# Neighbourhood attention with grid tokens in column order: two local key tiles per query tile, batches of two units, new bias layout

## The reference

```python
def neighbourhood_mixer(h_lat, h_ctx, p, need_ctx):
    ...
    kr = min(NA_ROWS_MAX, rows)                    # 8
    ...
    row_start = jnp.clip(r_idx - kr // 2, 0, rows - kr)
    col_start = jnp.clip(col - NA_COLS // 2, 0, GRID_W - NA_COLS)
    col_in = (col[None, :] >= col_start[:, None]) & (col[None, :] < col_start[:, None] + NA_COLS)
    ...
        s_loc = jnp.einsum('bqhd,brkhd->bhqrk', q_row, k_band).astype(jnp.float32) * ATTN_SCALE
        row_off = r0 + jnp.arange(kr) - r + NA_ROWS_MAX - 1
        bias = rpb[:, row_off][:, :, col_bias_idx].transpose(0, 2, 1, 3)
        s_loc = jnp.where(col_in[None, None, :, None, :], s_loc + bias[None].astype(jnp.float32), -jnp.inf)
        s_ctx = jnp.einsum('bqhd,bkhd->bhqk', q_row, k_c).astype(jnp.float32) * ATTN_SCALE
        s_all = jnp.concatenate([s_loc.reshape(B, NA_HEADS, GRID_W, n_loc), s_ctx], axis=-1)
        prob = jax.nn.softmax(s_all, axis=-1).astype(v_band.dtype)
        p_loc = prob[..., :n_loc].reshape(B, NA_HEADS, GRID_W, kr, GRID_W)
        o = (jnp.einsum('bhqrk,brkhd->bqhd', p_loc, v_band)
             + jnp.einsum('bhqk,bkhd->bqhd', prob[..., n_loc:], v_c))
...
    y_l = o.swapaxes(0, 1).reshape(B, S, D_MODEL) @ w_o
```

## Time and profile before

| | us |
|---|---|
| median of 3 runs | 3770.7 |
| lowest and highest | 3765.78, 3772.08 |
| span of the profiled execution | 3767.7 |
| TensorE busy in it | 3632.9 |
| VectorE, ScalarE, GpSimd busy | 2181.4, 1367.4, 830.9 |
| first scores of the neighbourhood attention, from the span's start | 1265.63 |
| its first transposes | 1276.84 |
| its last result written | 1426.8 |
| first matmul of the product behind it | 1429.22 |

### The profile page before, as it was taken

One profiled execution on the slowest core, in us unless ns is written; L12 is line 12 of the kernel. 1 busy time (PEld: TensorE's weight loads), 2 busy tenths in 40 slices (PEclk: granted clock), 3 DMA queues, 4 the chain that ended last, 5 costly groups with the idle time before them and its releaser, 6 DMA issues. The chain is left out here.

```text
span 3767.7 us, 53849 instructions
## 1 busy us (share of the span) xinstructions
PE 3632.9 (96%) x20043; PEld 2976.8 (79%) x20043; DVE 2181.4 (58%) x3423; ACT 1367.4 (36%) x2405; POOL 830.9 (22%) x588
## 2 busy tenths in 40 slices
PE   7999999999999999999999999999999998999998
PEld 5876788888878777777787888888878876687886
DVE  5748756566573564444436666556566628856445
ACT  4347541221243574222327622121224334523222
POOL 1500013223132111222220012213110008901222
PEclk9999999999999999999999999999999999999999
DMA  5234223332222212444310023323321240032322
GB/s 188 67 123 135 68 90 118 107 116 101 105 79 68 79 46 90 156 156 156 114 59 12 13 83 118 117 90 116 117 67 45 67 160 14 21 123 90 100 97 70
DMA packets 191993, 352.37 MB, mean 94 GB/s; under 512 B 42236, under 2 KB 43853, under 8 KB 191821
## 3 DMA queue, kind: packets, MB, share of 16 engines
q1 hardware_dynamic: 187693, 340.83, 27.4%
q10 hardware_dynamic: 4144, 9.44, 0.7%
HBM read 341.71 MB, written 16.92 MB: 95 GB/s over the span
## 5 line engine op out<-in xcount | busy, mean ns | idle before, releaser
L591 POOL TENSOR_TENSOR x<-x,scaled_buf 128x512 f32<-128x512 f32 (+1 forms) x360 | 493.4, 1387 | 2125.7 <-DVE scaled_buf L583 2125.1
L129 DVE TENSOR_TENSOR w_lo<-raw,w_hi 128x2048 fp32r<-128x2048 f32 x198 | 466.1, 2354 | 679.9 <-ACT w_hi L123 671.1
L123 ACT ACTIVATE w_hi<-raw 128x2048 fp32r<-128x2048 f32 x197 | 377.2, 1915 | 1286.4 <-PE psum L404 1284.0
L402 PE MATMUL psum<-hT_hi,w_hi 128*128 128x512 f32 (+1 forms) x1888 | 668.4, 354 | 2.9 <-issue 1.7
L403 PE MATMUL psum<-hT_lo,w_hi 128*128 128x512 f32 (+1 forms) x1888 | 665.1, 352 | 0.0
L404 PE MATMUL psum<-hT_hi,w_lo 128*128 128x512 f32 (+1 forms) x1888 | 664.7, 352 | 0.0
L402 PE MATMUL psum<-w_hi,uT_hi 128*128 128x512 f32 x1280 | 503.1, 393 | 0.1
L404 PE MATMUL psum<-w_hi,uT_lo 128*128 128x512 f32 x1280 | 498.6, 390 | 0.0
L403 PE MATMUL psum<-w_lo,uT_hi 128*128 128x512 f32 x1280 | 498.1, 389 | 0.0
L583 DVE TENSOR_TENSOR scaled_buf<-psum,gate 128x512 f32<-128x512 f32 x360 | 244.9, 688 | 328.0 <-PE psum L404 285.1
L402 PE MATMUL psum<-w_hi,hT_hi 128*128 128x512 f32 x1072 | 420.0, 392 | 4.4 <-issue 3.3
(11 more groups left out here) (292 smaller groups left out, 4883.5 us busy)
## 6 DMA issues: line engine op xcount, KB each, us to landing
raw<-in_w_mlp SPq DMA_DIRECT2D x64, 1024.0 KB, 5.3
raw<-in_ff_w SPq DMA_DIRECT2D x64, 1024.0 KB, 5.2
mod_wide<-in_w_mod SPq DMA_DIRECT2D x32, 1536.0 KB, 8.6
mod_wide<-in_w_mod SPq DMA_DIRECT2D x8, 3072.0 KB, 10.5
raw<-in_ssm_w_in SPq DMA_DIRECT2D x20, 1024.0 KB, 5.1
mod_slab<-in_w_mod SPq DMA_DIRECT2D x8, 2048.0 KB, 8.3
raw<-in_a_w_qkv SPq DMA_DIRECT2D x12, 1024.0 KB, 5.3
raw<-in_b_w_qkv SPq DMA_DIRECT2D x12, 1024.0 KB, 5.2
```

Source lines behind the costliest of these rows:

```text
L123: act.activation(K.w_hi[h][:, :, :], K.raw[h][:, :, :], ACT.Copy).then_inc(K.hi_done.h, 1)
L129: dve.tensor_tensor(K.w_lo[h][:, :, :], K.raw[h][:, :, :], K.w_hi[h][:, :, :].bitcast(F32), ALU.subtract).then_inc(K.lo_done.h, 1)
L402: pe.matmul(out, hi_a, hi_w, start=first, stop=False, **check)
L591: pool.tensor_tensor(x, x, K.scaled_buf[:, j % 2, :], ALU.add).then_inc(K.added.h, 1)
```

## The change

Grid tokens of this layer are numbered column by column. ScalarE writes them so into `feat` in `operand_stage` (`by_columns`). A key tile is then 16 grid columns with their 8 rows. The query tiles are shifted by half a tile against them: query tile t of 1 to 3 is the second half of tile t - 1 and the first half of tile t, and tile 0 is the first 8 and the last 8 columns. The window of such a query tile lies in two key tiles: t - 1 and t, or 0 and 3 for tile 0. The halves are put in place as the turned queries are evacuated (`turned_between`, two pieces an item, all four tiles of a group turned first). The attention has a stage of its own: a unit has two local and two context key tiles, 512 columns a head and one PSUM bank; units go in batches of two, with a step of transposes of batch s, scores of s + 2, weighted values of s - 1. The bias has zeros for the context columns, and its layout in HBM has changed. The way back to token order is in `window_split_stage`, feature by feature, and the product behind it takes features in order (`SplitFeed`).

```diff
@@ operand_stage, ScalarE
-                    out = feat[:, k % 2, t0 * P:(t0 + n) * P]
+                    out, turned = feat[:, k % 2, t0 * P:(t0 + n) * P], bank[:, 0:n * P]
+                    if by_columns and c == 0:
+                        out, turned = out.rearrange("p (c r) -> p r c", r=N_ROWS), turned.rearrange("p (r c) -> p r c", c=GRID_W)
...
@@ start_stage, SP and VectorE
-            sp.wait_ge(K.cleared.h, 1)
-            sp.dma_start(K.rel_table[:, 1:1 + REL_ROWS, REL_AT:REL_AT + REL_COLS], rpb).then_inc(K.rel_loaded.h, 16)
+            sp.dma_start(K.rel_in[:, :, :], rpb).then_inc(K.rel_loaded.h, 16)
...
-            link(dve.tensor_scalar(K.rel_table[:, :, :], K.rel_table[:, :, :], -1.0, None, ALU.mult))
+            dve.wait_ge(K.cleared.h, 1)
+            for r in range(N_ROWS):
+                ins = dve.tensor_scalar(K.rel_table[r // 4][:, r % 4, REL_AT:REL_AT + REL_COLS, :],
+                                        K.rel_in[:, N_ROWS - 1 - r:REL_ROWS - r, :].rearrange("h k c -> h c k"), -1.0, None, ALU.mult)
+            link(ins)
...
@@ bias: skewing, loading, masking
+def skew_bias(K, sp, p):
+    for head in (2 * p, 2 * p + 1):
+        for q0, q1, col0, kind in ((0, BLOCK_COLS, REL_AT + N_ROWS - 1, 0), (0, HALF_COLS, 2 * REL_AT - 1, 1),
+                                   (HALF_COLS, BLOCK_COLS, N_ROWS - 1, 1)):
+            src = bass.AP(tensor=K.rel_dram.tensor, offset=(head * REL_STEP + col0) * N_ROWS,
+                          ap=[[REL_STEP, N_ROWS], [-N_ROWS, q1 - q0], [1, 2 * P]])
+            sp.dma_start(K.skewed[head, kind, q0:q1].rearrange("c r x -> r c x"), src).then_inc(K.rel_loaded.h, 16)
...
+        sp.dma_start(bias_of(K, p)[:, m, 0::2, :], K.skewed[2 * p + m].rearrange("a c r x -> (c r) a x")).then_inc(K.g_loaded[p % 2].h, 16)
...
+    g = bias_of(K, p)[:, :, 0::2, :]
+    for m in range(2):
+        ins = pool.tensor_tensor(g[:, m], g[:, m], K.window_mask[:, :, :], ALU.add)
...
@@ turn_stage: ScalarE (VectorE likewise)
+                    pool.memset(bias_of(K, p)[:, :, 1, :], 0.0)
...
-                    act.wait_ge(K.src_turned.h, st0 + i + 1)
+                    act.wait_ge(K.src_turned.h, st0 + (turned_first[i] if turned_first else i + 1))
+                    for part, out in pieces(dst):
+                        ins = act.activation(out, blocks(i, part), ACT.Copy, scale=scale)
...
@@ window_attention_stage, in place of attention_stage with bias=True
+    def keys_of(t):
+        return (4, 5, 0, 3) if t == 0 else (t - 1, t, 4, 5)
...
+            def scores(b):
...
+                            if half == 0:
+                                pe.wait_ge(*upto(K.s_read, 2 * (v - 2) + m + 1))
+                            k = K.qkv[rows, first:second + 1:second - first, D + p * P:D + (p + 1) * P]
+                            mm = pe.matmul(bank_of(i, m)[:, half * LOCAL:(half + 1) * LOCAL], K.qkv[rows, t, p * P:(p + 1) * P], k,
+                                           start=half == 0, stop=True, skip_group_check=True)
...
+            def turns(b):
+                for i in range(2):
+                    pe.wait_ge(*upto(K.p_done, 2 * (2 * b + i) + 2))
+                    for m in range(2):
+                        c = 4 * b + 2 * i + m
+                        pe.wait_ge(*upto(K.pt_read[0], c - 2))
+                        for n in range(4):
+                            mm = pe.transpose(turning(c)[:, n * P:(n + 1) * P], K.p_win[:, b % 2, i, m, n * P:(n + 1) * P], K.ident[:, :])
...
+            for s in range(-2, NB):
+                if s >= 0:
+                    turns(s)
+                if s + 2 < NB:
+                    scores(s + 2)
+                if s >= 1:
+                    weighted(s - 1)
...
+            for s in range(-1, NB):                      # ScalarE
+                if s >= 0:
+                    copied(s)
+                if s + 1 < NB:
+                    probabilities(s + 1)
...
+                        dve.tensor_tensor_reduce(K.p_win[:, b % 2, i, m, :], bank_of(i, m)[:, :], g, 1.0, 3e38, ALU.add, ALU.min,
+                                                 K.win_min[:, b % 2, i, m:m + 1]).then_inc(K.s_read.h, 1)
...
+            for s in range(-2, NB):                      # VectorE
+                if s >= 1:
+                    inverse_sums(s - 1)
+                if s + 2 < NB:
+                    minima(s + 2)
+                if s >= 1:
+                    finish(s - 1)
...
@@ window_split_stage, in place of split_stage
+            for k in range(KD):
+                for src, at in pieces(k):
+                    ins = act.activation(at(grid(K.hT_hi, k)), src, ACT.Copy)
+                ins.then_inc(K.feat_hi.h, 1)
+            gate_evacuations(K, act, mm0, 1)
...
+                for src, at in pieces(k):
+                    ins = dve.tensor_tensor(at(grid(K.hT_lo, k)), src, at(grid(K.hT_hi, k)).bitcast(F32), ALU.subtract)
```

More of the change, by code:

```diff
@@ L1608, in turn_stage @@
     bank = lambda i: K.bank[(i - len(items)) % 8]
+    blocks = lambda i, part: bank(i).rearrange("p (a b) -> p a b", a=4)[:, :, part]
+    pieces = lambda dst: dst if isinstance(dst, list) else [(slice(0, P), dst)]
     with engines(K) as block:
@@ L1671, in _ @@
                 if i % 2 == 1:
-                    dve.wait_ge(K.src_turned.h, st0 + i + 1)
-                    dve.tensor_scalar(dst, bank(i).rearrange("p (a b) -> p a b", a=4), scale, None, ALU.mult)\
-                       .then_inc(K.src_read[1].h, 1)
+                    dve.wait_ge(K.src_turned.h, st0 + (turned_first[i] if turned_first else i + 1))
+                    for part, out in pieces(dst):
+                        ins = dve.tensor_scalar(out, blocks(i, part), scale, None, ALU.mult)
+                    ins.then_inc(K.src_read[1].h, 1)
                 if i == 7:
@@ L1686, in turn_stage, with attention_stage @@
     K.src_read[1].n += len(items) // 2
-def attention_stage(K, units, q_of, k_of, values, out, diff=False, bias=False, sink=False, mod=None, squares=False, context=None):
+def attention_stage(K, units, q_of, k_of, values, out, diff=False, sink=False, mod=None, squares=False):
     nc = K.nc
@@ L1718, in attention_stage @@
     with engines(K) as block:
[L1719 to L1727 removed]
+        if mod:
             @block.sync
@@ L1842, in probabilities @@
                 u = units[v]
-                if bias or sink:
+                if sink:
                     act.wait_ge(K.nm_done.h, at(K.nm_done, v))
```

273 lines of the change are left out of this document (200 added, 73 removed).

## The result

The changed kernel takes 3720.85 us (median of 4 runs, 3719.49 to 3722.64) where the kernel before takes 3770.26 beside it (4 runs, 3765.78 to 3772.08): a ratio of 0.9872, 95% interval 0.986 to 0.9884, 49.4 us less. The forecast was 3720 (3711 to 3734). The profiled execution has a span of 3717.7 us against 3767.7.

The account below looks back on a forecast made before the run. TensorE, busy 96% of the span, was taken to bound the kernel. Terms of -49.5, -4.8, +2.4, +0.2, +1.1 and +0.2 sum to -50.4: 3767.7 becomes 3717.3, plus 3.0 for the runs' median gives 3720 us, range 3711 to 3734.

Parts of the forecast that it names:

- Loop: Neighbourhood attention, first transposes to last result: TensorE sets the pace, 100.4 us where 149.9 stood, -49.5 us.
- hand-over: Attention loop: the fourth chunk of transposes waits for ScalarE's first bank copy, 0.1 us per batch, 1.6 in all.
- upper bound given for the period: Attention loop: two units' time scaled in plain proportion, changeovers too, 6.35 us against 6.2 by pieces.
- Fill: First scores to first transposes of the attention: 6.4 us against 11.2, with 1.5 charged for the lower clock, -4.8 us.
- Turn stage: Before the attention: scores wait for all evacuations, query tiles written in two pieces, +2.4 us, between +1.2 and +3.
- Start: Before layer 0: one VectorE operation on the bias table becomes eight, +1.1 us, bounds +0.5 and +3.
- Input stage: ScalarE writes the token order by columns for eight features; only the first delays the product, +0.2 us.
- rival 2: Input stage and split: scattered column writes are slow, four times as long, +3 and +4 us, 3727; chance 0.13.
- Split: After the attention: operands come feature by feature, the gate covers most of the first, +0.2 us, bounds 0 and +1.
- Rival 1: Attention loop: the banks pace it, hand-over 0.6 us a batch rather than 0.1, 8 more, 3728; chance 0.12.
- Rival 3: Attention loop: pauses keep TensorE at the half clock, 99 us more, 3819; chance 0.01.
- Rival 5: Cheaper yet: no half clock in the fill and no hand-over wait, -3 us and a little, 3716; chance 0.15.

Follow-up runs that it names:

- the extra copies: Changed kernel with one or three extra ScalarE copies into a spare buffer after each batch's four exponentials: 3723.8 us with one, 3734.2 with three.
- the copy in front: Changed kernel with one extra ScalarE copy into a spare buffer ahead of the first of each batch's four bank copies: 3729.8 us.
- the masks moved: Kernel before, with GpSimd's masks of the second and third head pair moved from the turn stage into the attention stage: ratio 1.0001.

## Why the prediction was right, and where it was not

- **Loop, -49.5 forecast, -50.3 measured.** Right by its own steps: transposes 1.91 + 0.1 hand-over (1.99), scores 1.95 (1.93), weighted 1.80 (1.80), inverse 0.54 (0.53), period 6.3 (6.25). That TensorE sets the pace is shown by the extra copies, that the hand-over stands exactly at its edge by the copy in front. The 0.8 us missed lie in the period, 6.25 against 6.3, sixteen times; the ends came out as charged. The second turn starts 0.35 late and the third another 0.49 (periods of 4.27 and 6.74), together the 0.8 of the sum, and the last weighted group waits 1.08 for 1.2. The upper bound given for the period, 6.35, should be 6.40 by its own rule; nothing hung on it.
- **Fill, -4.8 forecast, -6.4 measured.** The step that failed is the charge of 1.5 us for a lower clock: the clock stayed at 1.00 from the first scores on, and its last pause, 1.63 us just before them, did not lower it. The 4.9 of the sum before that charge was right (4.82). The reason given for before's length was wrong in its weight: the operation of 2.75 us accounted for 1.04, the rest is the three groups in one set of banks and the half clock. What the prediction did not see is that the same operation stood in the loop of before five more times.
- **Turn stage, +2.4 forecast, +1.6 measured.** Mechanism as forecast: the scores wait for all of VectorE's items, and its late low part sits in front of them. The size was off because the stretched low part fell from 3.02 to 2.60 us, as the lower bound had allowed, and the high part came 0.6 late, not 0.9. The terms named also add up to 2.3, not 2.4.
- **Start, +1.1 forecast, +2.9 measured.** The mis-sized term is the eight operations: 0.52 us each and 4.14 together, not 0.29 and 2.3. The price was taken from a 128-column read of PSUM in contiguous order; these read SBUF with a step of 31 words over 16 partitions. The +3 of the range held it.
- **Input stage, +0.2 forecast, +1.1 measured.** This is rival 2's mechanism at a small size: 1.74 times as long, not four. The Trainium skill, "Advanced Engine Details and Errata", memory cachelines, says that a new 16-byte line at each element costs a penalty; by that rule the written side had to be slower, and the traces agree, with 1353 against 778 ns. The step that failed is the claim that only the first feature delays the product. In the table above 0.5 of it is hidden, because layer 0 ran that much shorter: the profile of before has the half clock behind layer 0's attention (0.58 from 446 to 450 us), that of after has not.
- **Split, +0.2 forecast, -0.1 measured.** The pieces did get slower than charged, ScalarE's 384 columns with a step of 64 words 916 ns and 128 columns 436, but the gate covers the first and 2.7 us of product each later one. For the first it does so with nothing to spare: its low part ended 2.26 us after the last result, at 1377.36, where 1.6 had been charged, and the product started at 1377.46. The rows, in order of the two engines:

```profile
L2175 ACT ACTIVATE hT_hi<-qkv 128x384 fp32r<-128x384 f32 x8 | 7.3, 916 | 0.0
L2184 DVE TENSOR_TENSOR hT_lo<-qkv,hT_hi 128x384 fp32r<-128x384 f32 x8 | 7.1, 887 | 0.0
```

- **The rivals.** Rival 1 (banks pace the loop) did not come about, but the copy in front shows how near it was: half a microsecond later on ScalarE would have been its 8 us. Rival 2 was there in kind and cost 1.1 instead of 7. Rival 3's half clock did not occur in the loop. Rival 5 is half true: no half clock in the fill, the hand-over wait as charged.
- **The range.** Its lower end, 3711, lies 9 below the forecast, though the text puts the terms at about 7 and those it names add up to 4.9. The measured 3720.85 did not test it.

## What to carry to other kernels

Cost a loop that one engine paces from the piece lengths and changeovers of that engine's timeline, and then test the room of the others by where in their turn the room is: 1.39 us of idle time meant nothing for the copy that frees a bank. The small terms go wrong where work stands outside the steady state: operands turned ahead, the head of a pipeline, a serial chain before the first product; look there for who waits, not at the average. Before a gain or a loss in untouched code is put down to an edit, compare the granted clock of the same stretch of work in both profiles. When ScalarE must change an order on the way from PSUM to SBUF, try the step on the side that reads PSUM: here it cost nothing.

## What the runs showed of the hardware

- A 512-column f32 ScalarE operation from PSUM lasts 1353 ns with a step of 8 words on its SBUF output, 778 with a step of 64 words on its PSUM input, 779 with none.
- The sign of the bias table on GpSimd, 16 x 248 with the step of 31 words, where VectorE took 0.52: 1.04 us apart while VectorE was nearly idle, up to 3.4 while VectorE worked, and two of VectorE's own operations beside them grew from 0.75 to 0.93 and from 1.23 to 1.61.
- TensorE came to the half clock in before's fill with or without the 2.75 us stall (0.50 from 1273 to 1277 with the masks moved), so the stall was not needed for it. Before the fall TensorE had paused there for 1.14 us twice, with 2.5 us of work between.
- After the same pause of 2.44 us before the product behind layer 0's attention, the granted clock fell to 0.50 in six of twelve profiles and stayed at 1.00 in six. In the kernel with the sign on GpSimd the fall goes with 1.6 us against the kernel after.
- Eight transposes at the start, 32.8 to 34.8 us in the kernel after, follow each other every 0.21 us at a granted clock of 1.00; in the attention they follow every 0.11 at the same reading.
- Code that is the same in twelve profiles differed by up to 7.5 us in 2340, so single edits of 1 us had to be read from stretches.
